# The first RMS norm of a two-layer decoder step, moved from a block of its own into the first projection round

## What is computed

```python
def even_project(x, g_norm, w_in, b_f, g_q, g_k, pos):
    B, L, _ = x.shape
    h = rms_norm(x, g_norm)                       # x * rsqrt(mean(x*x) + eps) * g, over 1024 columns
    p = jnp.einsum('bld,dc->blc', h, w_in)
    fq, fk, fv, ff, fg, rq, rk, rv, rg = _split(p, EVEN_COLS)
...
    rq = rope(rq.reshape(B, L, H_RET, RET_DK), pos)
    rk = rope(rk.reshape(B, L, H_RET, RET_DK), pos) * (RET_DK ** -0.5)
```

## Time and profile before

| | us |
|---|---|
| median of three executions | 2396.11 |
| lowest and highest of them | 2395.28, 2398.52 |
| the profiled execution | 2399.81 |
| its span in the trace | 2398.0 |
| PE busy in it | 2234.9 (93%) |

### The profile page before, as it was taken

One profiled execution on the slowest core, in us unless ns is written; L12 is line 12 of the kernel. 1 busy time (PEld: TensorE's weight loads), 2 busy tenths in 40 slices (PEclk: granted clock), 3 DMA queues, 4 the chain that ended last, 5 costly groups with the idle time before them and its releaser, 6 DMA issues. The chain is left out here.

```text
span 2398.0 us, 30917 instructions
## 1 busy us (share of the span) xinstructions
PE 2234.9 (93%) x11248; PEld 1814.9 (76%) x11248; DVE 994.5 (41%) x1511; ACT 914.9 (38%) x1460; POOL 624.6 (26%) x380
## 2 busy tenths in 40 slices
PE   6999999899999887999999799699999999998999
PEld 5999999777777665777777478577777778886787
DVE  4333444353845746777777710411022222222211
ACT  4233333223534433767777510422223443334200
POOL 1223211220201000455666642031111221113300
PEclk8999999999999988999999899799999999999999
DMA  6122222302201122999999643323221223223531
GB/s 160 30 51 54 55 50 55 83 22 63 60 3 45 26 75 71 353 330 328 331 326 323 198 157 112 136 94 115 75 95 56 74 93 107 93 74 97 177 105 52
DMA packets 257404, 287.95 MB, mean 120 GB/s; under 512 B 69563, under 2 KB 168765, under 8 KB 257149
## 3 DMA queue, kind: packets, MB, share of 16 engines
q1 hardware_dynamic: 240538, 252.78, 33.4%
q10 hardware_dynamic: 16738, 33.53, 3.8%
HBM read 246.03 MB, written 41.26 MB: 120 GB/s over the span
## 5 line engine op out<-in xcount | busy, mean ns | idle before, releaser
L226 PE MATMUL bank<-whi,x_hi 128*128 128x512 f32 (+1 forms) x1536 | 592.7, 386 | 21.4 <-POOL wlo L206 16.3
L228 PE MATMUL bank<-wlo,x_hi 128*128 128x512 f32 (+1 forms) x1536 | 579.3, 377 | 0.0
L230 PE MATMUL bank<-whi,x_lo 128*128 128x512 f32 (+1 forms) x1536 | 578.9, 377 | 0.0
L226 PEld LDWEIGHTS bank<-whi,x_hi 128*128 128x128 f32 x1536 | 292.8, 191 | 83.4 <-POOL wlo L206 21.0
L259 ACT ACTIVATE projected<-bank 128x512 f32<-128x512 f32 (+1 forms) x160 | 92.1, 576 | 620.4 <-PE bank L230 591.5
L230 PEld LDWEIGHTS bank<-whi,x_lo 128*128 128x128 f32 x1536 | 292.6, 190 | 41.8
L228 PEld LDWEIGHTS bank<-wlo,x_hi 128*128 128x128 f32 x1536 | 293.6, 191 | 39.3 <-issue 0.7
L2165 POOL TENSOR_TENSOR dec_v_lo<-dec_v,dec_v_hi 128x1024 fp32r<-128x1024 f32 x92 | 238.5, 2609 | 197.7 <-ACT dec_v_hi L2522 197.7
L206 POOL TENSOR_TENSOR wlo<-wraw,whi 128x512 fp32r<-128x512 f32 (+1 forms) x192 | 230.5, 1233 | 31.5 <-ACT whi L199 31.4
L2337 DVE TENSOR_TENSOR dec_kt_lo<-bank,dec_kt_hi 128x512 fp32r<-128x512 f32 x256 | 168.9, 684 | 85.3 <-ACT dec_kt_hi L2512 84.4
L2512 ACT ACTIVATE dec_kt_hi<-bank 128x512 fp32r<-128x512 f32 x256 | 144.4, 592 | 106.0 <-PE bank L2193 105.2
(11 more groups left out here) (357 smaller groups left out, 3448.4 us busy)
## 6 DMA issues: line engine op xcount, KB each, us to landing
dec_k<-cache_k SPq DMA_DIRECT2D x256, 256.0 KB, 4.0
dec_v<-cache_v SPq DMA_DIRECT2D x256, 256.0 KB, 4.2
wraw<-w_in_even SPq DMA_DIRECT2D x32, 512.0 KB, 6.7
wraw<-w_in_odd SPq DMA_DIRECT2D x16, 1024.0 KB, 8.5
gv<-projected ACTq DMA_DIRECT2D x4, 2304.0 KB, 8.0
gm_v<-gv SPq DMA_DIRECT2D x8, 1152.0 KB, 6.0
m<-gm_mt ACTq DMA_DIRECT2D x8, 1056.0 KB, 4.1
wraw<-w_in_odd SPq DMA_DIRECT2D x4, 2048.0 KB, 8.4
```

What stands on the lines that cost most here:

```text
L226: pe.matmul(bank[:, 0:width], e.xhi[:, k, c:c + P], e.whi[:, k, 0:width], start=(k == 0), stop=False)
L228: pe.matmul(bank[:, 0:width], e.xhi[:, k, c:c + P], e.wlo[:, k, 0:width], start=False, stop=False)
L230: mm = pe.matmul(bank[:, 0:width], e.xlo[:, k, c:c + P], e.whi[:, k, 0:width], start=False, stop=(k == KD - 1))
```

## The change

The constants' block is now emitted behind the setup of the attention block, by a function `constants_first`, and takes three more DMAs. `norm_block` is no longer called for layer 0 (layer 1 keeps it). Its work is done by a new `first_norm` whose pieces are called at places inside the retention stage; the tiles are normed in `ORDER`. Its buffers lie in tensors that the retention stage uses later: the three slots in the second `projected` tensor, `xn` in `rot` and `sc`, the gain in `qk`, the squares in `m`, the sums and roots in `z`, `ab` and `ex`. Its transposes use banks 4 to 7, two per tile. The core of the diff:

```diff
+    def loads(sp):
+
+        load(sp, 0)
+        sp.dma_start(g, g_dram.partition_broadcast(P)).then_inc(g_landed.sem, 16)
+        load(sp, 1)
+
+    def more_loads(sp, weights, next_weights):
+
+        load_weights(sp, e, weights)
+        load(sp, 2)
+        for n in range(3, TT):
+            sp.wait_ge(xn_ready.sem, xn_ready.at(n - 3, 1))
+            load(sp, n)
+            if n == 6:
+                next_weights()
...
+        for n in range(TT):
+            steps = Chain(dve_steps, n)
+            dve.wait_ge(root_ready.sem, root_ready.at(n, 1))
...
+            dve.scalar_tensor_tensor(xn[n % 2][0:rows(n)], x[n % 3][0:rows(n)], rs[0:rows(n), n:n + 1], g[0:rows(n)],
+                                     ALU.mult, ALU.mult).then_inc(xn_ready.sem, 1)
+            if n > 0:
+                low(n - 1)
+        low(TT - 1)
...
     def sync(sp):
+        opening.more_loads(sp, retention_weights(e, a, 0), lambda: sp_weights(sp, e, 1, retention_weights(e, a, 1)))
         for dst, src in ((cos, a["c_cos"]), (sin, a["c_sin"]), (decay, a["c_decay"]), (decay_s, a["c_decay_s"]),
...
         for r in range(H):
-            if r + 1 < H:
+            if 0 < r and r + 1 < H:
                 sp_weights(sp, e, r + 1, retention_weights(e, a, r + 1))
...
         pool_split(pool, e, 0, RW)
         pool.memset(prefix[:, 0, :], 0.0).then_inc(cleared.sem, 1)
+        opening.wait_slots(pool)
+        pool.memset(pbs[1][:, 0, :], 0.0).then_inc(e.pb_cleared.sem, 1)
...
+        for n in range(2):
+            opening.turn(pe, n)
         for r in range(H + 1):
             for n in range(TT):
+                if r == 0:
+                    opening.wait_tile(pe, n)
                 if r < H:
                     pe_tile(pe, e, r, n, RW)
                 else:
                     after.tile(pe, n)
+                if r == 0 and n + 2 < TT:
+                    opening.turn(pe, n + 2)
...
         step, forget = [None], Chain(steps_f, 0)
+        opening.normed(dve)
         dve.wait_ge(table_landed.sem, table_landed.at(0, 16))
...
+        opening.root(act, 0)
+        opening.root(act, 1)
+        opening.hi(act, 0)
         act_split(act, e, 0, RW)
...
         for r in range(H + 1):
             for n in range(TT):
+                if r == 0 and n + 1 < TT:
+                    opening.hi(act, n + 1)
+                if r == 0 and n + 2 < TT:
+                    opening.root(act, n + 2)
...
                 sp.dma_start(e.ident[:], a["c_ident"]).then_inc(cst.sem, 16)
                 sp.dma_start(e.tri[:], a["c_tri"]).then_inc(cst.sem, 16)
+                loads(sp)
                 sp.wait_ge(cst.sem, cst.at(0, 32))
...
-            norm_block(nc, e, "norm0", tokens(xp, xs), a["norm_even"][0],
-                       lambda sp: load_weights(sp, e, retention_weights(e, a, 0)))
```

More of the change, by code:

```diff
@@ L559, in retention_stage @@
     t3, t4 = (qk[:, :, i, :].rearrange("p t (a f) -> p t a f", a=2) for i in range(2))
+    flat = lambda t_: t_[:].rearrange("p t c -> p (t c)")
+    later = flat(pbs[1])
+    opening = first_norm(e, tiles_src, a["norm_even"][0], [later[:, D * i:D * i + D] for i in range(3)],
+                      [rot[:].rearrange("p t a d -> p (t a d)")[:, 0:D], flat(sc)], flat(m)[:, 0:D], qk[:].rearrange("p t a f -> p (t a f)")[:, 0:D],
+                      flat(z)[:, 0:TT], flat(ab)[:, 0:TT], flat(ex)[:, 0:TT])
     places = [Places(TURN_M_AT, TURN_AT, TURN_AT + 1, TURN_AT + 2, TT - 1)] * H + [Places(2, 3, 4, 5, 6)]
@@ L643, in sync @@
         for r in range(H):
-            if r + 1 < H:
+            if 0 < r and r + 1 < H:
                 sp_weights(sp, e, r + 1, retention_weights(e, a, r + 1))
-            else:
+            if r + 1 == H:
                 sp.wait_ge(e.w_ready.sem, e.w_ready.at(H, 0))
@@ L653, in gpsimd @@
     def gpsimd(pool, after):
-        for x in pbs:
-            pool.memset(x[:, 0, :], 0.0).then_inc(e.pb_cleared.sem, 1)
+        pool.memset(pbs[0][:, 0, :], 0.0).then_inc(e.pb_cleared.sem, 1)
         pool.memset(o[:, 0, :], 0.0).then_inc(cleared.sem, 1)
@@ L1026, in scalar @@
             for n in range(TT):
+                if r == 0 and n + 1 < TT:
+                    opening.hi(act, n + 1)
+                if r == 0 and n + 2 < TT:
+                    opening.root(act, n + 2)
+                if r == 1 and n == 0:
+                    act.wait_ge(e.pb_cleared.sem, e.pb_cleared.at(0, 2))
                 if r < H:
@@ L1061, in scalar @@
         return lambda: store_m(H - 1)
-    return RetentionEnd(mb, use_out, use_state_s, e.s_sum, gate_taken), sync, gpsimd, tensor, vector, scalar
+    return (opening.loads, RetentionEnd(mb, use_out, use_state_s, e.s_sum, gate_taken), sync, gpsimd, tensor, vector,
+            scalar)
 FW = 4 * P
@@ L2088, in attention_block @@
         out_sync, out_scalar, out_gpsimd, out_tensor, out_vector = first_out
+        constants_first(ret_loads)
         def block_of(page):
@@ L3274, in build, with constants_first, _ @@
         cst = c.begin("constants_landed", 16 * 2)
[L3275 to L3280, removed]
-            @block.vector
-            def _(dve):
-                dve.memset(e.ones[:], 1.0)
-                dve.memset(e.eps[:], EPS)
-                dve.memset(e.one[:], 1.0)
-            @block.gpsimd
-            def _(pool):
-                pool.memset(e.q_own[:], 0.0)
-                for sem, value in c.primed:
-                    pool.sem_inc(sem, value)
-        c.close(1)
+        c.close(1)
+        def constants_first(loads):
+            with nc.Block() as block:
+                @block.sync
+                def _(sp):
+                    sp.dma_start(e.ident[:], a["c_ident"]).then_inc(cst.sem, 16)
+                    sp.dma_start(e.tri[:], a["c_tri"]).then_inc(cst.sem, 16)
+                    loads(sp)
+                    sp.wait_ge(cst.sem, cst.at(0, 32))
+                @block.vector
+                def _(dve):
+                    dve.memset(e.ones[:], 1.0)
+                    dve.memset(e.eps[:], EPS)
+                    dve.memset(e.one[:], 1.0)
+                @block.gpsimd
+                def _(pool):
+                    pool.memset(e.q_own[:], 0.0)
+                    for sem, value in c.primed:
+                        pool.sem_inc(sem, value)
         def tokens(prompt, sample):
```

81 lines of the change are left out of this document (76 added, 5 removed).

## The result

| | before | after |
|---|---|---|
| median, us | 2396.11 | 2383.83 |
| lowest and highest of five executions, us | 2394.82, 2398.52 | 2380.29, 2386.91 |
| profiled execution, us | 2399.81 | 2386.91 |
| its span, us | 2398.0 | 2384.8 |

The ratio of the times is 0.9946, with a 95% interval from 0.9935 to 0.9958: the change saves 12.3 us. 2383.4 was predicted. The profiled executions differ by 12.9 us.

A forecast was written before the change was run, and what follows sets the result against it. PE, busy 93% of the span, was taken as the bound, leaving only the start to gain: -20.6 (weights) + 1.9 (second tile) + 6.0 (six turns) = -12.7 us, so 2396.11 becomes 2383.4 us; range 2380 to 2391.

The forecast's parts named there:

- the held product: Third tile's DVE product in round 0, expected to wait from 21.7 to 24.3 us, until POOL's eight instructions were through.
- the clock: PE's clock at the start: read as granted in full until about 21 us, then half; 1.00 forecast from the second tile.
- The weights: First head's weights, requested at about 3.67 instead of 24.23 us: rounding starts at 15.5 instead of 36.11, 20.6 us earlier.
- The second tile: Round 0's second projection tile: starts at 26.9 us, 1.9 us behind a free PE, cutting the lead to 18.7.
- I take the same here: Round 0's third-tile product assumed kept out through POOL's whole row, as in round 1 of the earlier trace, until 24.3 us.
- The prediction's sum by the page: Alternative for round 0: DVE slips in after one POOL instruction, POOL ends 1.28 us later, second tile some 0.4 us later.
- The turns: Six more turns between round 0's tiles, taken as 0.96 us each from round 2: 6.0 us added on the path.
- The chain of ACT and DVE: Norm work beside round 0's tiles: 4.9 us against PE's 5.25 per tile, some 0.4 us to spare, costing nothing.
- the rival by which this chain sets the pace: ACT and DVE, not PE, pace round 0: 4.2 us more, 2387.6 us; chance 0.13.
- The rival of one or two slow tiles: Half clock for one or two tiles early in round 0, 4.4 us per tile: 2388 to 2392 us; chance 0.10.
- The cover: Head 2's weights, requested at 91 us behind the page copies, land at 101, needed at 112: 11 us spare, no cost.
- The lead is kept to the end: From round 1 on PE stays busy in the same order, so the 12.7 us lead lasts to the end.

The follow-up runs named there:

- e1: Kernel after with the first head's weights requested behind the rows of five tiles instead of two: median 2391.44 us, ratio to before 0.9974.
- e2: Kernel before with only the first head's weights requested early, behind two tiles and the gain, the norm still its own block: 2402.21 us, ratio 1.0024.
- e5: Kernel after with a plain contiguous DVE product of 1024 columns added ahead of round 1's first product: one execution took 2380.68 us.
- e10: Kernel after with two short single-input DVE row sums ahead of round 1's first product, so it is issued later in POOL's row: one execution 2383.29 us.
- e11: Kernel after with 36 unused transposes of the identity added on PE ahead of the first tile: one execution took 2384.08 us.
- e4: Kernel after with DVE's product for the third tile split into a plain two-tensor product and a scaling: median 2383.48 us, ratio 0.9945.
- e6: Kernel after with the low parts of the first head's weights stored by DVE instead of POOL: median 2383.69 us, ratio 0.9941.
- e9: Kernel after with first head's low parts on DVE, second tile finished before the weights, added PE transposes, and weights in two halves: 2378.65 us, ratio 0.9924.

## Why the prediction was right

The sum held, and most of its steps. Two readings of rows were wrong, the held product and the clock, and two prices too high, those of the second tile's start and of a turn.

*The weights.* 15.5 us was predicted for the first `whi`, 15.39 measured. In the place of the barrier stands the DMA as the releaser, and e1 shows that this wait is the one that counts. The other half of it is the norm inside the round: with the early request alone (e2) the kernel loses 5.4 us.

*The second tile.* 26.9 was predicted, 26.35 measured, but by another way. The step that failed is "I take the same here": the product of the earlier trace rows, held to the end of POOL's row, was taken for the one of round 0. It was let in, at a cost of 0.9 us to POOL and 0.3 us to DVE. So it was no longer DVE that came last but POOL and the turn: last matmul at 25.38, turn at 25.56, next tile at 26.35. The Trainium skill (SBUF — State Buffer, Who interferes with whom), by which two such instructions exclude each other until the first ends, so that DVE slips in after one of POOL's, describes round 0. The trace of round 1 (5.16 us, and 5.62 and 3.06 in e5 and e10) does not agree with it. The prediction's sum by the page, some 0.4 us behind 26.9, came out 0.9 us too late all the same: it charged POOL's row 1.28 us for the product (0.92 measured), began that row some 0.4 us too late (15.99 measured) and took 1.0 us for the turn (0.79 from its start to the next tile). That the held product had a counterpart that was let in stood in the trace of before, at 455.63.

*The turns.* 1.0 us each was taken from the earlier trace rows; measured are 19.26 us of lead at the second tile and 14.01 at `wlo` of head 1, so 5.25 us for six, 0.87 each. From 30.72 to 31.51 it is 0.79: the row's 1.03 us reaches to the end of the last transpose, and the next matmul starts before that. The term was 0.75 us too large. With the 0.55 us of the second tile that is the 1.3 us by which the lead at round 1 is larger than the 12.7 of the sum.

*The chain of ACT and DVE* fits, with less slack than claimed. A product ends 0.57 us ahead of the turn that reads it (30.15 and 30.72), but the second `low` behind it ends at 31.36, only 0.15 us ahead of the tile that waits for it (31.51), against 0.4 in the prediction. PE stands idle for neither, so the rival by which this chain sets the pace is out.

*The clock.* The conclusion held, the reading didn't. The prediction said that the clock was granted in full until about 21 us. In after the column reads 1.00 in each window up to 70 us, yet the matmuls at 17.62 and 17.95 stand 0.33 us apart, the spacing of half clock, and the turn at 10.37 took 1.97 us; from 21.5 on they stand 0.18 apart. In the earlier trace rows the same turn, 1.97 us at 32.38, stands where the column reads 0.50. So a 1.00 ahead of the first change in the column says nothing, and the first turns of both kernels ran at half clock. In before two turns from 13.17 on took 3.76 us, the one at 18.71 took 1.10, and from 21.30 on they took 1.97 again:

```profile
13.17 3.76 PE L418 MATMUL bank<-ident,norm_xn 128*128 128x128 f32 x16 [1.47 <-DVE norm_xn L403]
18.71 1.10 PE L418 MATMUL bank<-ident,norm_xn 128*128 128x128 f32 x8 [1.77 <-DVE norm_xn L403]
```

So there the clock rose during the norm, under turns alone, before it fell at about 21 us; the prediction's "granted in full until about 21 us" holds for the turn at 18.71 and not for those from 13.17. The Trainium skill (TensorE: Matmul & The Clock Gate, Part 1) has the throttled clock as the default that activity releases, and these spacings agree with it; the prediction was wrong to say that the first ten microseconds contradict it. The misreading cost nothing because in after the clock rose during the first tile, which POOL paces (e11). The rival of one or two slow tiles was met once, in e4: of the 2.1 us lost at round 1 there, 0.45 stand in POOL's longer row, and the rest goes with matmuls and a turn at half clock, where the prediction had 4.4 for each tile.

*SP.* The queue ran ahead of the forecast: the copies of pages began at 61.32 instead of 66, head 2's weights were requested at 85.96 instead of 91, and `whi` at 110.25 waited for PE. The cover held.

*"The lead is kept to the end."* True to some 3 us. It wanders from 16.0 to 10.8 and back to 13.2 (table above), where both kernels do the same work in the same order. The largest step, at the start of decoding, goes with a lower granted clock. The windows between the key loads and the next `m<-fox_o`, of before and of after:

```profile
848.00:944.00 96.00, 75.06 (x384) 60.44 (x384) 54.09 (x80) 29.59 (x55) 1.81 (x7) 0.86 0.13 44
```

```profile
833.40:933.20 99.80, 77.44 (x386) 60.91 (x385) 54.41 (x80) 29.50 (x55) 1.81 (x7) 0.81 0.12 43
```

The same 80 DVE, 55 ACT and 7 POOL instructions take 96 us at a granted clock of 0.86 and 99.8 at 0.81, and the 3.8 us between them are about the step from 14.5 to 10.8. Over the twelve traces this stretch has two lengths: 96.2 to 96.5 us at a granted clock of 0.84 to 0.86 (before, e2, e4, e5, e6), and 99.0 to 99.9 at 0.81 to 0.83 (after and the others). Kernels with the new start stand in both groups, so this step is not the change's. Whether the clock makes the stretch long, or the longer waits the clock low, is not tested. That the times of one kernel lie up to 6.6 us apart (2380.29 to 2386.91) is of the same size. So 14.0 us at round 1, 13.2 in the spans and 12.3 in the medians are one gain seen through this wander, and that 2383.83 lies within 0.5 us of 2383.4 is partly luck.

## What to carry to other kernels

A stage that stands ahead of everything is worth dissolving into the first round of the next one, if the request for that round's weights goes ahead of the remaining rows in the same change: alone, the early request made this kernel slower. The price is then counted in what it puts between the dense tiles, here 0.87 us per tile, and in whichever engine prepares the first tile. Moving that preparation to the faster engine, keeping PE busy ahead of it and cutting the load into pieces took another 5.3 us off the start of round 1 (e9); at the end that is likely and not settled. Read the clock at a program's start from the spacing of equal matmuls, not from the clock's column.

## What the runs showed of the hardware

- DVE's product of two SBUF tensors against a row of eight POOL instructions: let in within 0.3 us in round 0, in either form (1.59 us for 1.28 of work), held to the row's end in round 1, early or late in the row, strided or contiguous (5.16, 5.62, 3.06 us). In all twelve traces it is let in where POOL stood idle ahead of the row, and held where the row follows directly on another two-tensor instruction of POOL; the cause was not tested.
- The granted clock reads 1.00 ahead of its first change, while matmuls start every 0.33 us.
- Transposes alone raise the clock (a turn of 1.97 us down to 1.09 in e11, where PE had done nothing else). It didn't last: PE then idled until POOL's first `wlo`, and the first tile's matmuls came at half clock again.
- The same kind of request, five weight DMAs, took the queue 7.54 us to issue at 3.51 us, 6.99 at 30.56 and 4.26 at 85.96; what makes the difference was not tested.
- Storing 128x392 as a rounded rest took 0.49 us on DVE (3.90 for eight) and 0.99 on POOL (7.95).
